# Expert picks by groups of four, norms by tile and half, and one norm at the block boundary

## The reference

```python
aff = softmax(h @ w_router)                    # 256 tokens x 16 experts
gate, idx = top_k(aff.T, 32)                   # each expert takes 32 tokens
xe = h[idx]                                    # 16 x 32 x 1024
ye = (silu(xe @ w_gate) * (xe @ w_up)) @ w_down
out = zeros.at[idx].add(gate * ye)
```

## Time and profile before

| | |
|---|---|
| median of 3 runs | 3415.31 us (3412.54 to 3419.99) |
| profiled execution, its time | 3414.24 us |
| its span, first to last instruction | 3412.4 us |
| TensorE busy | 2596.0 us, 76% |
| VectorE busy | 1360.4 us, 40% |
| ScalarE busy | 861.2 us, 25% |
| GpSimd busy | 565.0 us, 17% |
| mean granted TensorE clock | 0.905 |
| moved by DMA | 1101.82 MB |

### The profile page before, as it was taken

The page is one execution under the profiler, slowest core; times in us unless marked ns, Lnnn a source line. Parts: engine busy times, 40 slices in busy tenths (PEclk is TensorE's granted clock), DMA queues, the critical chain, the costliest instruction groups (busy, mean ns, idle before and its releaser), DMA issues. The chain is left out here.

```text
span 3412.4 us, 30496 instructions
## 1 busy us (share of the span) xinstructions
PE 2596.0 (76%) x10510; PEld 1322.6 (39%) x10510; DVE 1360.4 (40%) x3271; ACT 861.2 (25%) x2246; POOL 565.0 (17%) x549
## 2 busy tenths in 40 slices
PE   7997665655999756565577987878888788977776
PEld 6774211112777312121263733335453354533222
DVE  0352000001143200000124577765866658567774
ACT  1230000000122110000122143453633536334333
POOL 0000000000000000000001144432424324244342
PEclk9998868888999878888787999999999898999999
DMA  7342899999433399999720699999999989899997
GB/s 270 119 144 99 338 410 410 410 409 401 156 144 133 121 409 408 408 409 409 304 99 8 241 422 421 421 383 357 406 374 408 368 350 390 343 420 421 421 421 331
DMA packets 257145, 1101.82 MB, mean 323 GB/s; under 512 B 15424, under 2 KB 28256, under 8 KB 191456
## 3 DMA queue, kind: packets, MB, share of 16 engines
q1 hardware_dynamic: 181536, 559.83, 42.6%
q0 software_dynamic: 73728, 536.90, 38.2%
q10 hardware_dynamic: 1728, 3.14, 0.2%
HBM read 1095.64 MB, written 4.19 MB: 322 GB/s over the span
## 5 line engine op out<-in xcount | busy, mean ns | idle before, releaser
L1067 PE MATMUL ps<-wbuf,ar 128*128 128x512 f32 x2048 | 983.3, 621 | 193.9 <-ACT ar L1642 193.4
L808 PE MATMUL ps<-wbuf,ar 128*32 128x512 f32 x3072 | 495.1, 783 | 375.1 <-DMA wbuf<-in_w_expert_up 151.8
L1591 DVE CUSTOM_DVE_ANT_0 ar<-wbuf,Y 128x1024 f32<-128x1024 f32 x512 | 627.4, 1225 | 339.6 <-DMA wbuf<-in_puv,ar 330.0
L2023 POOL DMA_INDIRECT wbuf<-in_puv,ar x512 | 544.4, 1063 | 962.3 <-PE ps L1067 894.3
L1067 PEld LDWEIGHTS ps<-wbuf,ar 128*128 128x128 f32 x2048 | 379.5, 197 | 747.2 <-issue 745.7
L604 PE MATMUL ps<-HT,wbuf 128*128 128x256 f32 (+2 forms) x2656 | 497.5, 347 | 14.2 <-DMA wbuf<-in_w_mem_kv 5.4
L604 PEld LDWEIGHTS ps<-HT,wbuf 128*128 128x128 f32 (+1 forms) x2656 | 433.6, 191 | 77.0 <-issue 10.1
L1642 ACT ACTIVATE ar<-ar 128x1 f32<-128x1 f32 (+3 forms) x1052 | 270.1, 257 | 598.1 <-DVE ar L1591 563.2
L808 PEld LDWEIGHTS ps<-wbuf,ar 128*32 128x32 f32 x3072 | 99.7, 129 | 755.3 <-issue 214.4
L2013 POOL TENSOR_TENSOR sm<-sm,co 128x2 f32<-128x2 f32 x9 | 6.2, 693 | 1794.2 <-DVE sm L1102 1794.2
L1639 ACT COPY ar<-ps 128x512 f32<-128x512 f32 (+2 forms) x130 | 71.4, 549 | 790.2 <-PE ps L808 361.6
(11 more groups left out here) (132 smaller groups left out, 1481.7 us busy)
## 6 DMA issues: line engine op xcount, KB each, us to landing
wbuf<-in_w_expert_gate SPq DMA_DIRECT2D x64, 2048.0 KB, 24.1
wbuf<-in_w_expert_up SPq DMA_DIRECT2D x64, 2048.0 KB, 24.1
wbuf<-in_w_expert_down SPq DMA_DIRECT2D x64, 2048.0 KB, 24.0
wbuf<-in_w_in SPq DMA_DIRECT2D x22, 2048.0 KB, 11.3
wbuf<-in_peer_w_q SPq DMA_DIRECT2D x12, 2048.0 KB, 14.0
wbuf<-in_w_o SPq DMA_DIRECT2D x6, 2048.0 KB, 9.6
wbuf<-in_b_w_in SPq DMA_DIRECT2D x6, 2048.0 KB, 13.3
wbuf<-in_w_branch_b SPq DMA_DIRECT2D x4, 2048.0 KB, 12.6
```

Source lines behind the costliest of these rows:

```text
L808: m = T.e.matmul(ps(jobs[n])[32 * k:32 * k + 32, :], lhs(c, k), v[:, k, 512 * n:512 * n + 512], start=(c == 0), stop=(c == 7), tile_positi ...
L1067: m = T.e.matmul(acc[n][:, :], DG[:, j % 4, :], rows_of(name)[:, 1024 + 512 * n:1536 + 512 * n], start=(j == 0), stop=(j == 127))
L1591: V.did(V.e.tensor_tensor_reduce(JK, rows_of(f"g{l}{i}.{j}")[:, 0:1024], Y[:, i, :], 1.0, 0.0, ALU.mult, ALU.add, DT[:, i, j:j + 1]), f"do ...
L2023: G.land(G.e.indirect_dma_start(out=rows_of(name), out_offset=None, in_=I["puv"], in_offset=bass.IndirectOffsetOnAxis(ap=IX[:, i, j:j + 1] ...
```

## The change

- **Picks by groups.** The picks are made per group of four experts, with two banks a group that hold four chunks of 128 columns each. `PA` is built for the first four experts, then for the other twelve. The first group's picks come ahead of `gate_up(0)`, the other three and the transposes of the places behind it.
- **Norms by tile and half.** Squares are summed by tile and half (`square`), each tile has its own mean and power, VectorE scales half 0 of each tile and ScalarE half 1, and the transposes are by tile: tile 0's two banks are brought out by ScalarE in eight instructions of 128 columns, tile 1's by VectorE in two of 512. Where a norm follows a residual, each square waits only for its own add, and tile 0 is scaled ahead of the last add.
- **Residual products** wait for the merges chunk by chunk; `MT` moves out of `Y`, and the third mixer's `aOT` too.
- **The router** is made with its own weights as the stationary side, 16 x 256, then copied and transposed.
- **One norm at the boundary.** With each add of the last group VectorE makes `Y` = `X` times the closing gains, ScalarE sums the squares of both, and `row_norms` works out both norms' factors from the sums; `X` and `Y` are then scaled from `Y`.
- **Order of loads.** x ahead of the constants; the memory input and its weights one group later, and `row.final` with them.

```diff
-        MT = Y[:, :, :].rearrange("p i (c t) -> p (i c) t", t=256)
+        MT = arv(2048, 4096, "p (c t) -> p c t", c=8)
...
-                    if g == 0 and l:
-                        S.wait_ge(*at["x1.xe7"])
+                    if g == 1 and l:
+                        S.wait_ge(*at["x1.xe3.1"])
                         S.land(S.e.dma_start(Y[:, :, :], I["mem_2"][0].rearrange("(i p) n -> p i n", p=P)),
                                landed["mem"], count, "mem.in")
-                    if l and g:
-                        load(f"mem.w{g - 1}", I["w_mem_kv_2"][g - 1], 8, 512) if g < 3 else None
+                        row("row.final", "final")
+                    if l and g > 1:
...
             def norm(p):
-                T.wait_ge(*at[f"{p}.a"])
-                T.wait_ge(*at[f"{p}.b"])
-                to_T(p, Y, 8)
+
+                for i in range(2):
+                    T.wait_ge(*at[f"{p}.a{i}"])
+                    T.wait_ge(*at[f"{p}.b{i}"])
+                    for k in range(2):
+                        b = take(f"{p}.t{i}{k}")
+                        for n in range(4):
+                            m = tr(b[:, 128 * n:128 * n + 128], Y[:, i, 512 * k + 128 * n:512 * k + 128 * n + 128])
+                        T.did(m, f"{p}.t{i}{k}")
 
             def turned_in(p):
-                T.wait_ge(*at[f"{p}.t4.out"])
-                T.wait_ge(*at[f"{p}.t6.out"])
+                for i, k in HALVES:
+                    T.wait_ge(*at[f"{p}.t{i}{k}.out"])
...
-            def residual(p, lhs):
+            def residual(p, lhs, made):
+
                 for half in range(2):
                     v = tile(f"{p}wo{half}")
                     for i in range(2):
-                        proj_N(f"{p}r{half}{i}", v, i, 0, 512, *([f"{p}wo{half}.used"] if i else []), lhs=lhs)
+                        b = take(f"{p}r{half}{i}")
+                        for c in range(8):
+                            T.wait_ge(*at[made[c]])
+                            m = T.e.matmul(b[:, :], lhs[:, c, 128 * i:128 * i + 128], v[:, c, :], start=(c == 0), stop=(c == 7))
+                        T.did(m, f"{p}r{half}{i}", *([f"{p}wo{half}.used"] if i else []))
...
+                b = take(p + "rl")
+                T.did(mm(b[0:16, 0:256], [(wr[:, c, :], HT[:, c, :]) for c in range(8)]), p + "rl")
+                T.wait_ge(*at[p + "rl.out"])
                 b = take(p + "rt", keep=True)
                 for i in range(2):
-                    m = mm(b[:, 16 * i:16 * i + 16], [(HT[:, c, 128 * i:128 * i + 128], wr[:, c, :]) for c in range(8)])
+                    m = tr(b[:, 16 * i:16 * i + 16], rtT[:, 128 * i:128 * i + 128])
...
+                def pick(g):
+
+                    T.wait_ge(*at[f"{p}pa{min(g, 1)}"])
                     for k in range(2):
-                        for i in range(2):
-                            m = tr(b[:, 256 * k + 128 * i:256 * k + 128 * i + 128], PG[:, i, 128 * (g + k):128 * (g + k) + 128])
-                    T.did(m, f"{p}pt{g}")
-                T.wait_ge(*at[p + "pt0.out"])
-                T.wait_ge(*at[p + "pt2.out"])
+                        b = take(f"{p}xe{g}.{k}")
+                        for n in range(4):
+                            c = 4 * k + n
+                            m = mm(b[:, 128 * n:128 * n + 128], [(Y[:, i, 128 * c:128 * c + 128],
+                                                                  PA[:, i, 128 * g:128 * g + 128]) for i in range(2)])
+                        T.did(m, f"{p}xe{g}.{k}")
+
+                def places():
+                    T.wait_ge(*at[p + "pg"])
+                    for g in (0, 2):
+                        b = take(f"{p}pt{g}")
+                        for k in range(2):
+                            for i in range(2):
+                                m = tr(b[:, 256 * k + 128 * i:256 * k + 128 * i + 128],
+                                       PG[:, i, 128 * (g + k):128 * (g + k) + 128])
+                        T.did(m, f"{p}pt{g}")
...
                 def gate_up(g):
+                    for k in range(2):
+                        T.wait_ge(*at[f"{p}xe{g}.{k}.out"])
...
+                pick(0)
                 for g in range(4):
                     gate_up(g)
+                    if g == 0:
+                        for n in range(1, 4):
+                            pick(n)
+                        places()
                     next(extra, None)
...
+            def mean_a(p, i, n=1024):
+                V.wait_ge(*at[f"{p}.ss{i}0"])
+                ts(part[:, i:i + 1], sums[:, i, 0:1], 1.0 / n, 1e-6, ALU.mult, ALU.add)
+
+            def mean_b(p, i, n=1024):
+                V.wait_ge(*at[f"{p}.ss{i}1"])
+                ts(rstd2[:, i:i + 1], sums[:, i, 1:2], 1.0 / n, part[:, i:i + 1], ALU.mult, ALU.add, f"{p}.ms{i}")
+
+            def scaled(p, i, src=X):
+
+                V.wait_ge(*at[f"{p}.r{i}"])
+                ts(half_of(Y, i, 0), half_of(src, i, 0), rstd2[:, i:i + 1], None, ALU.mult, None, f"{p}.a{i}")
+
+            def gained(p, gname):
+
+                g0 = PF[gname][0]
+                for k in range(2):
+                    job = f"{p}.t1{k}"
+                    V.wait_ge(*at[job])
+                    tt(HT[:, 4 * k:4 * k + 4, 128:256], ps(job)[:, :].rearrange("p (k t) -> p k t", k=4),
+                       pf[:, g0 + 4 * k:g0 + 4 * k + 4].unsqueeze(2).to_broadcast([P, 4, 128]), ALU.mult, job + ".out")
+
+            def norm(p, gname, src=X):
+                for i in range(2):
+                    mean_a(p, i)
+                    mean_b(p, i)
+                for i in range(2):
+                    scaled(p, i, src)
...
-            def residual(p):
+            def residual(p, nxt, gname):
+
                 for half in range(2):
                     for i in range(2):
                         V.wait_ge(*at[f"{p}r{half}{i}"])
-                        x = X[:, i, 512 * half:512 * half + 512]
+                        x = half_of(X, i, half)
                         tt(x, x, ps(f"{p}r{half}{i}")[:, :], ALU.add, f"{p}r{half}{i}.out")
+                        if (half, i) == (1, 0):
+                            mean_a(nxt, 0)
+                            mean_b(nxt, 0)
+                            mean_a(nxt, 1)
+                            scaled(nxt, 0)
+                mean_b(nxt, 1)
+                scaled(nxt, 1)
+                gained(nxt, gname)
...
-                for i in range(2):
-                    tt(PA[:, i, :].rearrange("p (e c) -> p e c", e=16), C("iota").unsqueeze(1).to_broadcast([P, 16, 32]),
-                       ky[:, i, :].unsqueeze(2).to_broadcast([P, 16, 32]), ALU.is_equal, *([p + "pa"] if i else []))
+                for e0, e1 in ((0, 4), (4, 16)):
+                    for i in range(2):
+                        tt(PA[:, i, 32 * e0:32 * e1].rearrange("p (e c) -> p e c", c=32),
+                           C("iota").unsqueeze(1).to_broadcast([P, e1 - e0, 32]),
+                           ky[:, i, e0:e1].unsqueeze(2).to_broadcast([P, e1 - e0, 32]), ALU.is_equal,
+                           *([f"{p}pa{min(e0, 1)}"] if i else []))
+
+                def pick(g, k):
+                    job, g0 = f"{p}xe{g}.{k}", PF[f"norm_ffn{l}"][0] + 4 * k
+                    V.wait_ge(*at[job])
+                    tt(XE[:, 4 * k:4 * k + 4, 128 * g:128 * g + 128], ps(job)[:, :].rearrange("p (c n) -> p c n", c=4),
+                       pf[:, g0:g0 + 4].unsqueeze(2).to_broadcast([P, 4, 128]), ALU.mult, job + ".out")
+
+                pick(0, 0)
+                pick(0, 1)
                 for i in range(2):
                     tt(PG[:, i, :].rearrange("p (e c) -> p e c", e=16), PA[:, i, :].rearrange("p (e c) -> p e c", e=16),
...
-                               *([p + "end"] if (g, i, n) == (3, 1, 1) else []))
+                    for i, n in HALVES:
+                        V.wait_ge(*at[f"{p}y{g}.{i}{n}"])
+                        x = half_of(X, i, n)
+                        tt(x, x, ps(f"{p}y{g}.{i}{n}")[:, :], ALU.add, f"{p}y{g}.{i}{n}.out",
+                           *([p + "end"] if (g, i, n) == (3, 1, 1) else []))
+                        if g == 3 and l:
+                            tt(half_of(Y, i, n), x, gb[:, 512 * n:512 * n + 512], ALU.mult, f"fin.y{i}{n}")
 
                 for g in range(4):
                     gate_up(g)
+                    if g == 0:
+                        for m in range(2, 4):
+                            pick(m, 0)
+                            pick(m, 1)
+                        V.wait_ge(*at[p + "pt2"])
+                        copy(PT[:, 2:4, :], two(ps(p + "pt2")[:, :]), p + "pt2.out")
                     next(extra, None)
                     if g:
                         down(g - 1)
                     V.wait_ge(*at[f"{p}tn{g}.4"])
...
-            def row_norm():
-                r = small(8, 2)
-                rstd("fin", r, 1024)
-                V.wait_ge(*at["row.final"])
-                for i in range(2):
```

(73 more changed lines are left out.)

179 lines of the change are left out of this document (74 added, 105 removed).

## The result

The changed kernel takes 3362.51 us (median of 4 runs, 3355.56 to 3370.27) where the kernel before takes 3415.03 (4 runs, 3412.54 to 3419.99) beside it: a ratio of 0.9845, 95% interval 0.9816 to 0.9874, 52.5 us less (the interval of the ratio leaves 43 to 63 us). The forecast was 3362.7. The profiled execution of the changed kernel spans 3355.4 us; the one before spanned 3412.4.

What follows compares the result with a forecast made beforehand. Serial chains ahead of self-paced stages, such as the weight-streaming expert stages, were taken as the bound. Terms 4.0 + 11.7 + 1.2 + 0 + 23.8 + 11.9 = 52.6 us off 3415.3 gave 3362.7 us, range 3351 to 3381.

Steps and rivals of the forecast that it cites:

- place matrix: Ahead of the first picks in both layers: two narrower instructions, gain 0.8 us, twice.
- residual per chunk: Residual products no longer wait for the last merge: gain 1.6 us twice, 0.85 in the third mixer, sum 4.0.
- Norm behind a residual: From the residual's last add to the next products: 5.9 us in place of 9.8, gain 3.9, three times.
- First picks: Only four experts' picks ahead of the first expert matmul: 7.1 us in place of 18.2, gain 11.1, twice.
- The other groups: Three later groups' picks behind the first gate and up products: bursts of 18.7 and 15.3 us, hidden by streaming.
- Cover: In the expert stages, how long six prefetched weight tiles keep the stream going during other TensorE work: 24 us.
- The passage to the third mixer: Last group's first add to the projection: 14.9 us in place of 28.1, gain 13.2 less 1.3.
- Loading x ahead of the constants: At the kernel's start: the first square waits for both loads, so the new order gains nothing.
- Router: New router form, both layers: between a gain of 2.6 us and a loss of 3.0 by clock, taken as nothing.
- bursts that outlast the ring: Rival: half clock in the later picks stops the stream 8.3 and 1.5 us; time 3372.5; chance 0.12.
- the dear narrow record: Rival, in the picks: a 128-column record costs as much as a wide one, 0.43 us; time 3426; chance 0.01.
- the expert stages did not start earlier: Rival: something other than the first used tile holds the weight queue; 17.9 us left, time 3397; chance 0.05.

Runs made afterwards that it cites:

- fillers: Changed kernel with TensorE's idle gaps in the norms behind a residual and in the routing filled with unread products of constants: 3352.17 us, 0.9818.
- VectorE on tile 0: Changed kernel with VectorE instead of ScalarE bringing out tile 0's transposed banks in the three norms behind a residual: 3367.59 us, 0.9844.
- both edits: Changed kernel with unread products of constants in TensorE's gaps and VectorE bringing out tile 0's banks: 3351.64 us, 0.9798.

## Why the prediction was right

The sum of 52.6 us stands against 53.0 at the first gather and 52.5 as a median; the mechanism is the one argued: everything between the mixers and the streams is a serial chain, and what leaves it passes through whole. That the sum came out to within half a microsecond is luck: single steps missed by up to 3.4 us either way, and the retrieval stages alone vary by 18 us. The order of the picks and the early row were taken back by an experiment each; the norms by tile and half, the place matrix and the residual per chunk were not, and their terms are read from the traces alone. The terms one by one:

- *Norm behind a residual*, 3.9 three times: 3.84, 3.84 and 4.06. Both the length (5.9 us from the end of the add) and what ends it (ScalarE's eight instructions, 3.17 us against 3.1) came as worked out.
- *First picks*, 11.1 twice: 12.1 and 10.0, together 22.0. The sum was right and the clock behind it was read right on average: mean 0.71 in layer 0 and 0.55 in layer 1, 5.3 and 6.7 us for the 6.2 estimated. The weight loads followed the clock: 32 of them are 3.65 us busy at 1.00 (fillers), 6.51 at 0.55. The Trainium skill (TensorE: Matmul & The Clock Gate, section LDWEIGHTS) gives a load as its columns over 1.2 GHz, with no term for the granted clock. The rows at 1.00 agree with it (0.114 us a load), those at 0.55 don't (0.203).
- *The other groups*, hidden: 16.4 and 12.7 us of burst instead of 18.7 and 15.3, since the clock stood at 1.00 from the burst's first record; the half-clock start that I took from the picks of before doesn't occur here, behind an up product. (It does dip in two other bursts: 96 records took 12.03 us in layer 0 with the fillers and 12.10 in layer 1 with VectorE on tile 0, for 10.98.) The sum of 18.7 had put the relative tables at 3.4 us where the row that it names shows 4.24; they took 3.69. Cover 24 us predicted, 22.7 to 24.5 measured.
- *Place matrix*, 0.8 twice: from the first use of the scores to the picks it is 12.95 and 12.94 us before, 12.14 and 12.13 after.
- *The passage to the third mixer*, 13.2 less 1.3: 13.1 less 1.0, the latter within what the stream varies.
- *Residual per chunk*: the waits of 1.58 us ahead of the products are gone. The stages they stand in are longer or shorter by as much for other reasons: from first projection to residual products layer 0's mixer takes 252.1 to 256.0 us over eleven profiled executions of kernels that don't differ there, and 255.4 before. The 3.4 us of the table, for 1.6 predicted, are that: the changed kernel's execution is at the low end. In the third mixer 1.8 us came for 0.85, because its 64 records took 29.61 us for 30.65.

Three terms were wrong, the first by 2.9 us one way, the other two by 2.1 and 2.5 the other:

- *"Loading x ahead of the constants: both are waited for by the first square, nothing."* It is 2.9 us. The step overlooked ScalarE's table load, which starts when x has landed and then lies in the wait for the constants, and that with x, the larger of the two loads, first the last landing comes 1.5 us earlier.
- *"Router: ... I take nothing."* In layer 0 it lost 2.4 us, within the bounds that were given, and in layer 1 it gained 0.3. The bound was the clock, and the old router, at 10.48 and 10.47 us for the new one's 10.68 and 10.17, shows that the form has next to no part in it.
- Not in the sum at all: *the projection for the retrieval* starts at half clock behind the thinner norm (0.74 on average in its first 9.7 us, and 7.24 us to its first bank became 9.71). It costs 2.5 us, and products in that norm's gaps give just that back. The Trainium skill has the general form of it (TensorE: Matmul & The Clock Gate, section HAM oscillation — how this bites in real kernels): idle gaps between bursts of products send the clock down, and the next burst pays. The fillers' row agrees (1.00 for 0.74).

Of the rivals, bursts that outlast the ring did not come (16.4 us against a cover of 24), and the dear narrow record did not either (10.98 us for 96 of them, 0.114 each). One slip in them decides nothing: if the expert stages did not start earlier, 17.8 us of the sum would be left, not 17.9.

The retrieval stages, 4.0 us shorter in the profiled execution, are no part of the gain: over twelve profiled executions the stretch from the first gather to the end lasts 1482.3 to 1500.1 us, with the same code. That is also why changes of 3 us at the first gather don't show as times. What makes this stretch vary was not tried.

## What to carry to other kernels

Before a stage that lasts as long as its bytes, do only the work that its first tile needs; the rest goes behind that tile, as long as it is shorter than the ring (here six tiles of 5.13 us, of which some 24 us were usable). Splitting work into four pieces was not dear in itself here: 128 columns took 0.114 us at full clock, and 512 took 0.43. Price the piece at the clock at which it will run. And look at what a shortened chain does to TensorE's clock: a gap with little work in it costs again at the first dense products behind it, and products of constants in the gaps bought back 12 us here.

## What the runs showed of the hardware that was not expected

- The stretch ahead of the first layer's experts got shorter by a third (46.6 us from the last add to the first expert product, now 32.3), and TensorE's clock in it did not rise: the router's 16 records took 6.31 us at 0.57, and 3.61 at 1.00 with fillers ahead of them.
- The fillers don't hold the clock at every place in every execution: with the fillers alone layer 0's picks ran at 1.00 (3.84 us) and layer 1's at 0.69 (5.46 us); with both edits layer 0's took 5.46 and layer 1's 3.84. Without fillers, too, the two layers trade places between executions (5.32 and 6.70 in one, 6.70 and 5.37 in another).
- ScalarE's table load (1.28 us) began when the first operand of its first instruction had landed, at 5.97 us, and not when all that it waits for had, at 9.66: so the order of two loads that one instruction needs decides whether the table load is hidden.
